# Turning the second head group's probabilities by a DRAM exchange and VectorE block transposes in steps 32 to 53

## What is computed

```python
def mixer_b(q, k, v, rel_table):
    ...
    logits = jnp.einsum('bcqhd,bckhd->bhcqk', qc, kb) * SCALE
    ...
    logits = logits + bias[:, None]
    valid = band_valid(nc, B_BAND)
    logits = jnp.where(valid[:, None, :], logits, NEG)
    p = jax.nn.softmax(logits, axis=-1)
    out = jnp.einsum('bhcqk,bckhd->bcqhd', p.astype(vb.dtype), vb)
```

## Time and profile before

| what | value |
|---|---|
| median of 3 runs | 1033.59 us (1033.16 to 1033.89) |
| span of the profiled execution | 1031.9 us |
| TensorE busy, of the span | 1023.0 us, 99% |
| VectorE busy | 770.9 us, 75% |
| ScalarE busy | 470.5 us, 46% |
| GpSimd busy | 219.7 us, 21% |

### The profile page before, as it was taken

The page is one execution under the profiler, slowest core; times in us unless marked ns, Lnnn a source line. Parts: engine busy times, 40 slices in busy tenths (PEclk is TensorE's granted clock), DMA queues, the critical chain, the costliest instruction groups (busy, mean ns, idle before and its releaser), DMA issues.

```text
span 1031.9 us, 15795 instructions
## 1 busy us (share of the span) xinstructions
PE 1023.0 (99%) x5525; PEld 851.0 (82%) x5525; DVE 770.9 (75%) x1506; ACT 470.5 (46%) x978; POOL 219.7 (21%) x218
## 2 busy tenths in 40 slices
PE   9999999999999999999999999999999999999997
PEld 8899887788778888878888888888888888888886
DVE  4955677867688578888988788786444777778997
ACT  6632355545477567836221221311344445454562
POOL 5200000000000003148675674761100000000000
PEclk9999999999999999999999999999999999999999
DMA  9835442111071474045444434446777733454344
GB/s 202 222 98 136 108 134 77 42 47 37 11 225 43 123 188 159 21 143 212 171 167 155 163 134 152 163 144 225 243 243 242 229 103 92 143 194 142 93 142 164
DMA packets 135071, 147.92 MB, mean 143 GB/s; under 512 B 72248, under 2 KB 85440, under 8 KB 132944
## 3 DMA queue, kind: packets, MB, share of 16 engines
q1 hardware_dynamic: 133920, 146.68, 45.7%
q10 hardware_dynamic: 688, 0.20, 0.1%
q0 software_dynamic: 384, 0.04, 0.0%
HBM read 103.65 MB, written 47.49 MB: 146 GB/s over the span
## 4 chain that ended last, share of the span: by engine, by line
PE 94%; DVE 3%; issue 1%; DMA 1%; ACT 0%; POOL 0%; DVEq 0%; ACTq 0%; POOLq 0%
PE ps L2242 27%; PE ps L2244 27%; PE ps L2243 27%; PE ps L2451 3%; PE ps L2465 3%; PE ps L2432 2%; PE ps L2376 1%; DVE wc_lo L1918 1%; PE ps L2411 1%; PE ps L2584 1%; PE ps L2586 1%; PE ps L2572 1%; DMA up_raw<-in_w_up 1%; DVE b_lo L1907 1%; PE ps L2254 0%
## 5 line engine op out<-in xcount | busy, mean ns | idle before, releaser
L2242 PE MATMUL ps<-b_hi,wc_hi 128*128 128x512 f32 x448 | 174.6, 390 | 0.5 <-DVE wc_lo L1918 0.5
L2243 PE MATMUL ps<-tm_lo,sm_hi 128*128 128x512 f32 (+1 forms) x450 | 174.6, 388 | 0.0
L2244 PE MATMUL ps<-tm_hi,sm_lo 128*128 128x512 f32 (+1 forms) x450 | 174.6, 388 | 0.0
L2242 PE MATMUL ps<-tm_hi,sm_hi 128*128 128x512 f32 (+1 forms) x450 | 174.6, 388 | 0.0
L2244 PE MATMUL ps<-b_hi,wc_lo 128*128 128x512 f32 x448 | 174.3, 389 | 0.0
L2243 PE MATMUL ps<-b_lo,wc_hi 128*128 128x512 f32 x448 | 174.3, 389 | 0.0
L1485 ACT ACTIVATE sm_hi<-sm_raw 128x512 fp32r<-128x512 f32 x112 | 70.7, 631 | 161.8 <-DMA sm_raw<-u_matrices 161.8
L2146 DVE TENSOR_TENSOR sm_lo<-sm_raw,sm_hi 128x512 fp32r<-128x512 f32 x112 | 77.4, 691 | 77.9 <-ACT sm_hi L1485 77.3
L2242 PEld LDWEIGHTS ps<-b_hi,wc_hi 128*128 128x128 f32 x448 | 84.1, 188 | 18.3 <-DVE wc_lo L1918 0.9
L2242 PEld LDWEIGHTS ps<-tm_hi,sm_hi 128*128 128x128 f32 x450 | 84.5, 188 | 17.6
L2244 PEld LDWEIGHTS ps<-tm_hi,sm_lo 128*128 128x128 f32 x450 | 84.5, 188 | 17.4
(11 more groups left out here) (261 smaller groups left out, 2063.2 us busy)
## 6 DMA issues: line engine op xcount, KB each, us to landing
u_matrices<-stage SPq DMA_DIRECT2D x112, 256.0 KB, 2.0
sm_raw<-u_matrices SPq DMA_DIRECT2D x112, 256.0 KB, 2.6
up_raw<-in_w_up SPq DMA_DIRECT2D x16, 1024.0 KB, 5.0
w<-in_w_down SPq DMA_DIRECT2D x64, 256.0 KB, 3.8
w_raw<-in_w_in SPq DMA_DIRECT2D x8, 512.0 KB, 3.5
xr<-in_x SPq DMA_DIRECT2D x8, 512.0 KB, 4.3
x_rows<-xr SPq DMA_DIRECT2D x8, 512.0 KB, 4.1
xf<-x_rows SPq DMA_DIRECT2D x8, 512.0 KB, 3.5
```

Of the source, the lines that this page charges most:

```text
L2242: pe.matmul(out, w_hi_, x_hi_, start=start, stop=False)
L2243: pe.matmul(out, w_hi_, x_lo_, start=False, stop=False)
L2244: return pe.matmul(out, w_lo_, x_hi_, start=False, stop=stop)
```

## The change

In steps 32 to 53 TensorE turns no probabilities. ScalarE now multiplies by the inverted sum, and writes the result in an order in which a plain store to DRAM and a plain load back put each 32x32 block on the partitions where VectorE's block transpose needs it. The store has four pieces of `keys_of(n)` x 128 bytes for each partition, the load `keys_of(n)` x 512 bytes for each. SP issues two stores and two loads a step, in `exchange_step`. There are three landing buffers, used in turn, one shared copy of the raw scores (slot 0 and 1 of `prob_b`) and one of the values to be stored (slot 2 and 3). VectorE turns step n-2 in step n, TensorE weighs step n-3 in step n. The turned queries lie in another order, which `weigh` undoes by a strided moving operand and a strided output. At steps 54 to 56 the old way takes over again: TensorE weighs 51, 52, then 53 and 54. Fill halves from the 22nd on alternate between two PSUM banks where they used one.

```diff
+            def exchange_step(n):
+                m = keys_of(n) * 32
+                for hh in range(2):
+                    q = turn_number(n, hh)
+                    sp.wait_ge(s_pb, pb0 + q + 1)
+                    sp.dma_start(pb_dram[q, 0:512 * m].rearrange("(a p m) -> p a m", a=4, m=m),
+                                 stored_probs(n, hh).rearrange("p (a m) -> p a m", m=m)).then_inc(s_pst[hh], 16)
+                for hh in range(2):
+                    q = turn_number(n, hh)
+                    sp.wait_ge(s_pst[hh], pst0[hh] + 16 * (n - A_STEPS + 1))
+                    if q == 0:
+                        sp.wait_ge(s_pv, A_STEPS)
+                    elif q >= 3:
+                        sp.wait_ge(s_tb, tb0 + q - 2)
+                    sp.dma_start(turn_in[q % 3][:, 0:keys_of(n)],
+                                 pb_dram[q, 0:512 * m].rearrange("(p k n) -> p k n", p=P, n=P)).then_inc(s_pld[q % 3], 16)
...
+            for n in range(A_STEPS, LATE):
+                exchange_step(n)
+                if n == A_STEPS:
+                    load_bias(5)
+                elif n % T == T - 1:
+                    sp.wait_ge(s_nm, 2 * n + 2)
+                    load_bias(n // T + 2)
+                elif n % 4 == 1 and n // 4 + 2 - A_STEPS // 4 + 4 < FILL_TILES:
+                    load_fill(n // 4 + 2 - A_STEPS // 4 + 4)
...
+            def normalize(n, hh):
+                at = 2 * (n % 2) + hh
+                act.wait_ge(s_ri, 2 * n + hh + 1)
+                if n > A_STEPS:
+                    act.wait_ge(s_pst[hh], pst0[hh] + 16 * (n - A_STEPS))
+                nc.scalar.activation(stored_probs(n, hh).rearrange("p (a k i) -> p k a i", a=4, i=32),
+                                     prob_of(n, hh)[:, first_column(n):].rearrange("p (k a i) -> p k a i", a=4, i=32),
+                                     ACT.Copy, scale=rinv[0][:, at:at + 1]).then_inc(s_pb, 1)
...
+            for n in range(A_STEPS, LATE):
...
+                for hh in range(2):
+                    exp(n, hh)
...
+                for hh in range(2):
+                    normalize(n, hh)
+                tiles_hi(halves_done(n - 1))
+                splits(n)
...
                 for hh in range(2):
                     slot = 2 * (n % 2) + hh
                     if hh == 0:
                         dve.wait_ge(s_qk, n + 1)
+                    if A_STEPS < n <= LATE:
+                        dve.wait_ge(s_pb, pb0 + turn_number(n - 1, hh) + 1)
+                    elif n == LATE + 1:
+                        dve.wait_ge(s_pst[hh], pst0[hh] + 16 * (LATE - A_STEPS))
...
+            def turn_probs(n, hh):
+                q = turn_number(n, hh)
+                dve.wait_ge(s_pld[q % 3], pld0[q % 3] + 16 * (q // 3 + 1))
+                dve.wait_ge(s_pv, n - 1)
+                nk = keys_of(n)
+                nc.vector.transpose(blocks(prob_t(n, hh)[:, 0:nk * P]), turn_in[q % 3][:, 0:nk]).then_inc(s_tb, 1)
...
+            for n in range(A_STEPS, LATE):
                 done = halves_done(n - 1)
                 take(done)
+                scores(n)
+                for hh in range(2):
+                    if n >= A_STEPS + 2:
+                        turn_probs(n - 2, hh)
+                    invert(n, hh)
+                take_low(done)
+                splits(n)
+
+            for n in range(LATE, STEPS + 1):
+                done = halves_done(n - 1)
+                take(done)
+                if n < STEPS:
                     scores(n)
                 if n == LATE:
                     take_low(done)
+                if n < LATE + 2:
+                    for hh in range(2):
+                        turn_probs(n - 2, hh)
+                copies_of(n - 1)
+                if n < STEPS:
                     for hh in range(2):
                         normalize(n, hh)
...
+                        out_ = ps[64 * hh:64 * hh + 64, weigh_bank(n), (t % 4) * P:(t % 4) * P + P]
+                        if turned_b(n):
+                            out_ = out_.rearrange("p (j c) -> p c j", c=4)
+                            probs = turned_query_blocks(n, hh)[:, k]
...
+            for n in range(A_STEPS, LATE):
+                if not (paired(n) and n % 2):
                     scores(n)
                 if paired(n) and n % 2 == 0:
                     scores(n + 1)
...
+                elif n >= A_STEPS + 3:
+                    weigh(n - 3)
+                first, end = filled(n - 1), filled(n)
                 for m in range(first, end):
...
                     fill(m)
+
+            for n in range(LATE, STEPS + 1):
+                if n < STEPS:
+                    scores(n)
+                for c in range(len(chunks_of(n - 1))):
+                    transposes(n - 1, c)
+                if n < LATE + 3:
+                    weigh(n - 3)
+                if n >= LATE + 2:
                     weigh(n - 2)
```

More of the change, by code:

```diff
@@ L231, in chunk_banks @@
         for c in range(len(chunks_of(n))):
-            if n >= LATE - 1:
-                bank = (6, 4, 5)[(len(banks) + A_STEPS // 2) % 3]
-            else:
-                bank = 6 if n < A_STEPS else 5 if paired(n) and n % T == 1 else (6, 5, 6)[c]
-            banks[n, c] = bank, last.get(bank)
+            bank = 6 if n < A_STEPS else (6, 4, 5)[len(banks) % 3]
+            banks[n, c] = bank, last.get(bank) if n < A_STEPS or len(banks) >= chunks_until(LATE) + 3 else None
             last[bank] = n, c
@@ L568, in build @@
         s_p = sem("probs_ready")
+        s_pb, pb0 = s_rowp, 1
+        s_tb, tb0 = s_rcol, 2
+        s_pst, pst0 = (s_tab, s_rep), (96, 144)
+        s_pld, pld0 = (s_x0, s_g1, s_rowst), (16, 16, 32)
         s_pt = sem("probs_transposed")
@@ L1262, in _ @@
                     store_first_mix(n)
[L1263 to L1268 removed]
+                for hh in range(2):
+                    normalize(n, hh)
+                tiles_hi(halves_done(n - 1))
+                splits(n)
+            for n in range(LATE, STEPS + 3):
+                if n == LATE + 1:
+                    store_mix(12)
+                elif n % 4 == 2 and n > LATE:
+                    store_mix((n - 6) // 4)
+                if n == LATE:
+                    tiles_hi(halves_done(n - 1))
+                if n < STEPS:
+                    for hh in range(2):
+                        exp(n, hh)
+                if n <= STEPS:
+                    for c in range(len(chunks_of(n - 1))):
                         if chunks_of(n - 1)[c][2]:
@@ L1821, in _ @@
                     take_low(done)
-                if n >= LATE or n == A_STEPS + 2:
-                    copies_of(n - 1)
-                if paired(n) and n % T == 2:
-                    scores(n + 1)
-                if n < STEPS and not (paired(n) and n % 2):
+                if n < LATE + 2:
+                    for hh in range(2):
+                        turn_probs(n - 2, hh)
+                copies_of(n - 1)
+                if n < STEPS:
                     for hh in range(2):
                         normalize(n, hh)
-                if n < LATE and n != A_STEPS + 2 and not paired(n - 1):
-                    copies_of(n - 1)
-                if paired(n) and n % T == 0:
-                    scores(n + 1)
-                if paired(n) and n % 2 == 0:
-                    for hh in range(2):
-                        normalize(n + 1, hh)
-                if paired(n) and n % 2:
-                    copies_of(n - 1)
-                    copies_of(n)
-                if n < LATE:
-                    take_low(done)
                 splits(n)
@@ L2348, in fill @@
                 elif k == 0:
-                    pe.wait_ge(s_et, scaled_when(m - (2 if m < SINGLE else 1)))
+                    pe.wait_ge(s_et, scaled_when(m - (1 if m == SINGLE else 2)))
+                    if m == SINGLE + 1:
+                        pe.wait_ge(s_pta, copies(A_STEPS - 1, True))
                 if m < V_HALVES:
@@ L2456, in weigh @@
                 nk = keys_of(n)
-                pe.wait_ge(s_pta, copies(n, True))
-                if copies(n, False):
-                    pe.wait_ge(s_ptd, copies(n, False))
+                if turned_b(n):
+                    pe.wait_ge(s_tb, tb0 + turn_number(n, 1) + 1)
+                else:
+                    pe.wait_ge(s_pta, copies(n, True))
+                    if copies(n, False):
+                        pe.wait_ge(s_ptd, copies(n, False))
                 if n % 4 == 0:
-                    pe.wait_ge(s_mix, n // 4 + 1)
+                    pe.wait_ge(s_mix, n // 4 + (n // 4 in (8, 13, 14, 15)))
                 at = P + P * (p - 4)
@@ L2491, in _ @@
                     fill(m)
-            for n in range(A_STEPS, STEPS + 1):
-                first, end = min(filled(n - 1), 8 * HALVES), filled(min(n, STEPS - 1))
-                if A_STEPS + 2 < n < LATE and n % 2:
-                    weigh(n - 3)
-                    weigh(n - 2)
-                if n < STEPS and not (paired(n) and n % 2):
```

(2 more changed lines are left out.)

137 lines of the change are left out of this document (59 added, 78 removed).

## The result

The changed kernel takes 1050.17 us (median of 4 runs, 1046.83 to 1053.24) against 1033.7 for the kernel before: a ratio of 1.0161, 95% interval 1.0139 to 1.0183. It is 1.6% slower, 24.6 us above the forecast of 1025.6 and outside its range.

What follows compares the result with a forecast made beforehand. TensorE, busy 99% of the span, was taken as the bound: 16.5 off, less 3.5 for waits and 5.0 for the handoff, gives 8.0 us off 1031.9, 1023.9; with 1.7 for the median 1025.6 us, range 1019.5 to 1034.5.

Steps and rivals of the forecast that it cites:

- no group stands at the transposes' line: Sign in TensorE's timeline, steps 32 to 53: the 160 transposes, 16.3 us, are gone.
- fills unbroken are 2.95 us: Sign on TensorE in the stretch: fills no longer cut in two; twelve steps lose the break, 1.0 us.
- a weighing is 1.24 alone: Sign on TensorE: steps weighed singly take 1.24 us each, ten costing 0.8 us more; 1.4 or more means stride costs.
- the stride: TensorE's weighing with strided operand and output: taken to cost 0, bounds 0 and 13 us.
- VectorE's turn: VectorE's block transpose of 640 columns in a step of five key tiles: taken as 0.84 us.
- TensorE's own sum: Steps 32 to 53: 16.3 us of transposes plus 1.0 of fill breaks less 0.8 of weighing, 16.5 us off.
- The waits of the order: Steps 38 to 41 and 46 to 49: `take_low` behind ScalarE's multiplications makes TensorE wait, 3.5 us, bounds 0 and 7.
- The handoff: Steps 54 to 57, no fills to cover waits: 10.55 us becomes 15.5, 5.0 given back, bounds 2 and 7.
- the exchange: Stores and loads back through DRAM, steps 32 to 53: land 1 to 2 us early and cost nothing.
- R = 2.6 + 3.1: Exchange round trip at 320 KB, store plus load: 5.7 us, bounds 2.1 + 2.6 and twice 5.2.
- the two-step loop: Turn n, inversion of n+2, multiplication, issue, store, load, turn n+2: 2.5 + R against 10.5 us, deciding from R = 8.
- Rival 2: The exchange is late and becomes the bound instead of the transposes: at R = 9.3, 16 us more, 1041.6; chance 0.13.

Runs made afterwards that it cites:

- pairs unblocked: SP's order made store (n,0), store (n,1), load (n-1,0), load (n-1,1), all else as in the changed kernel: 1057.95 us.
- opening the two-step loop: Against the changed kernel, VectorE inverts a head of step n before, not after, it turns that head of step n-2: 1051.37 us.
- free loads: Against the changed kernel, each exchange load reads as many bytes from a finished bias table and waits for no store: 1030.18 us.
- staggered kernel: Against the changed kernel, only SP's order changed, to store (n,0), load (n-1,1), store (n,1), load (n,0): 1037.91 us.

## Why the prediction was wrong

Right, by its own steps: no group stands at the transposes' line, fills unbroken are 2.95 us, a weighing is 1.24 alone (209.43 to 210.67), **the stride** costs nothing, as taken, and **VectorE's turn** measured 0.84 us for 640 columns, as taken. Without the exchange the kernel is 1.1% faster than before, so the work on the engines did come out as a gain.

Near in the sum, but not term by term, by the kernel without an exchange: **TensorE's own sum** went down by 15.2 us (busy 117.78 before, 102.57 there) where 16.5 was forecast. **The waits of the order** were 0.85 us (103.42 less 102.57) where 3.5 was; the lateness of `take_low` that was laid out by hand did not come. **The handoff** gave back 3.9 us (14.41 against 10.55) where 5.0 was forecast, but out of other parts: its waits are 2.7 us and not 5.8, and the ten transposes and the weighing behind them take 1.8 us more than before at the lower clock (281.02 to 285.27, 4.25 us, against 290.03 to 292.52, 2.49), for which the forecast had no term. The net, 10.1 us off the span against a forecast of 8.0, is near in part because these errors go both ways.

**The step that failed is the exchange**, which the forecast had landing 1 to 2 us early and costing nothing. It cost 27.4 us (1050.17 less 1022.74), at three points.

First, the term R = 2.6 + 3.1. The 2.6 was right for a store with no load issued shortly ahead (2.5 in the kernel with the pairs unblocked), the wrong value for one in this kernel: 4.8 in the median, 7.1 and 7.60 behind the weights. The loads took 3.7 to 4.0. R was 8.5, and about 9 with the second head's issue.

Second, the loop. The text asked from which R the two-step loop through the data decides, found 8, and counted for SP only issues of 0.64 us. It left out that SP *waits*: load (n) waits for store (n), and store (n+1) is behind it on the queue. With the buffer that ScalarE may only overwrite when the store has landed, that is a loop of one step with two halves: landing 4.8, then the load's issue 0.5 and the next store's 0.5, or the multiplication 0.8 and the store's issue 0.5, against a step of 5.27 us. By these numbers, an estimate, it decides from a landing of about 4, not from R = 8. The chain between 204 and 226 us shows this loop. For it speak also that opening the two-step loop gave nothing, that the free loads gave 20.0 us, and that SP's order alone gave 12.3. Opening one half alone, ScalarE's with the values in place or SP's with the stores on ScalarE, gave 2.2 and 3.0 us, which is within the noise; both halves hang on the same landing, so that is what the loop would have, but it shows nothing, and no run opened both at once. How much of the 12.3 is SP's waiting and how much the shorter flight (4.8 to 3.3 us for the first head, 5.0 to 4.3 for the second) stays open: the run meant to part them closed another loop.

Third, the clock, for which the forecast had no term. The granted clock fell to the 1.2 GHz level at waits of 4.94, 2.45 and 3.39 us in the stretch, and of 0.69 and 1.92 us in the handoff; it did not fall at one of 2.31 us before the scores at 203.11. In the handoff TensorE was busy for 16.04 us where it was for 10.20 before:

```profile
288.96:299.51 10.55, 10.20 (x122) 8.59 (x122) 8.49 (x33) 8.49 (x22) 0.00 (x0) 1.00 0.89 202
```

That is 5.8 us, of which little is other work. In the stretch, distances from start to start against the same ones at full clock give 2.6, 1.4 and 1.4 us. So TensorE's work takes some 11 us longer, an estimate. How much of the time that is isn't shown: no run held the clock up, and where TensorE would have waited for the exchange anyway, slower work fills the wait. In the staggered kernel, with shorter waits, the mean granted clock of the window is 0.99 and of the handoff 0.89 instead of 0.94 and 0.61.

Rival 2 said rightly that the exchange would be late, and had a chance of 0.13. Its 1041.6 us came from the two-step loop, which was not the one that binds, and it too had neither SP's waits nor the clock. Its condition was checked against transfers of the kernel before, while the change makes four a step and puts stores right behind loads.

The rule that was named beside rival 2 (the Trainium skill, "DMA: Bandwidth & Descriptors", Latency and other measured facts: latency grows at high load) is not borne out by the mean load: 214 GB/s in the kernel with free loads left a 320 KB store at 3.1 us, 179 GB/s in the changed kernel had it at 4.8. What was issued directly ahead of the store told more than the load on the whole; no run here shows the memory's latency by itself.

## What to carry to other kernels

When a store and a load back are put into a software pipeline, draw the loop through the *issuing queue* as well as the one through the data: a queue that waits for a landing in front of a load holds up the next store, and lets it go just behind the loads, where it flies longest. Put each wait for a landing behind an issue that is already due (here store, former load, store, load), and cut large loads that aren't urgent into pieces between them; but don't hold the loads back further than that. Cost a transfer by rows in which something was issued just ahead of it, on whichever queue, and look at what TensorE's clock does after the waits of some microseconds that a change brings in.

## What the runs showed of the hardware

- A store of 64 KB took 1.8 to 1.9 us at best, 320 KB 2.5, with another of 320 KB issued 0.7 to 0.9 us after it, which took 3.3. Issued 0.5 to 1.1 us behind loads of 320 KB it took 3.8 to 5.5, right behind 512 KB of weights 7.1 and 7.6 from the same queue, 8.6 with the weights issued from ScalarE's.
- A product with its moving operand in runs of 32 columns and its output on every fourth column took 0.062 us, as a plain one (1.24 us for 20).
- With pieces of 640 bytes instead of 2560 the median of the 320 KB stores was 4.7 us and not 4.3, in one trace each.
- The mean granted clock over the handoff was 1.00 before, with one wait of TensorE of 0.4 us; 0.89 in the staggered kernel, with waits of 1.4 and 2.0 us; and 0.61 in the changed kernel, with waits of 0.7, 1.9, 1.55 and 1.46 us.
